# Attention value products: high and low value weights side by side for two query blocks, halves added on VectorE, and an order of its own for the last head pair

## The reference, cut to what matters

```
def one_block(args):
    q_blk, fq_blk, pos_blk = args
    s = jnp.einsum("bqhd,bkhd->bhqk", q_blk, k, preferred_element_type=jnp.float32) * scale
    s = s + fq_blk[..., :, None] - fk_t[:, :, None, :]
    mask = kpos[None, :] <= pos_blk[:, None]
    s = jnp.where(mask, s, -jnp.inf)
    pr = jax.nn.softmax(s, axis=-1)
    return jnp.einsum("bhqk,bkhd->bqhd", pr.astype(v.dtype), v)
```

## Time and profile before

| | us |
|---|---|
| median of 3 runs (2857.04 to 2859.82) | 2859.51 |
| the profiled execution | 2863.89 |
| its span, first to last instruction | 2862.1 |
| attention, first value transposes of pair 0 to those of pair 7 | 584 |
| last pair, from there to the first matmul of the output projection | 77.4 |

### The profile page before, as it was taken

The page is one execution under the profiler, slowest core; times in us unless marked ns, Lnnn a source line. Parts: engine busy times, 40 slices in busy tenths (PEclk is TensorE's granted clock), DMA queues, the critical chain, the costliest instruction groups (busy, mean ns, idle before and its releaser), DMA issues.

```text
span 2862.1 us, 43282 instructions
## 1 busy us (share of the span) xinstructions
PE 2773.8 (97%) x18039; PEld 2699.5 (94%) x18039; DVE 1366.4 (48%) x1841; ACT 835.4 (29%) x1328; POOL 118.4 (4%) x82
## 2 busy tenths in 40 slices
PE   7999999999999999999999999879999999999998
PEld 7999999999999999988888888769999999999998
DVE  7676354244244344455556555554542442442444
ACT  6566221111111122334444444442211111110221
POOL 1000200000000000300000000002000000000000
PEclk9999999999999999999999999889999999999999
DMA  3112111111111111232222233111111111111112
GB/s 133 38 37 90 55 45 44 55 45 38 53 45 42 50 51 38 56 106 83 81 75 70 90 90 97 53 38 46 45 40 51 50 40 54 45 38 53 45 44 78
DMA packets 91341, 166.48 MB, mean 58 GB/s; under 512 B 18066, under 2 KB 55154, under 8 KB 91026
## 3 DMA queue, kind: packets, MB, share of 16 engines
q1 hardware_dynamic: 91154, 163.72, 18.9%
HBM read 141.60 MB, written 13.70 MB: 54 GB/s over the span
## 4 chain that ended last, share of the span: by engine, by line
PE 88%; DVE 4%; issue 4%; ACT 2%; DMA 1%; DVEq 0%; SPq 0%; ACTq 0%
PE psum L339 78%; PE psum L1151 2%; PE psum L1099 2%; PE psum L1123 2%; DVE SB L1551 1%; DMA NF<-nf_scratch 1%; PE psum L1081 1%; DVE PTL L1578 1%; PE psum L1138 1%; ACT PTH L879 0%; DVE X L1634 0%; PE psum L949 0%; ACT L695 0%; ACT SB L863 0%; PE psum L951 0%
## 5 line engine op out<-in xcount | busy, mean ns | idle before, releaser
L339 PE MATMUL psum<-XH,WH 128*128 128x352 f32 x2904 | 642.0, 329 | 1.7 <-issue 1.7
L339 PE MATMUL psum<-XL,WH 128*128 128x352 f32 x2904 | 627.5, 324 | 0.0
L339 PE MATMUL psum<-XH,WL 128*128 128x352 f32 x2904 | 627.1, 323 | 0.0
L321 ACT ACTIVATE WH<-WR 128x1024 fp32r<-128x1024 f32 (+2 forms) x217 | 215.4, 993 | 1037.1 <-PE psum L339 1025.1
L339 PEld LDWEIGHTS psum<-XH,WL 128*128 128x128 f32 x2904 | 498.0, 188 | 1.6
L339 PEld LDWEIGHTS psum<-XL,WH 128*128 128x128 f32 x2904 | 494.0, 188 | 1.6
L339 PEld LDWEIGHTS psum<-XH,WH 128*128 128x128 f32 x2904 | 489.9, 190 | 4.9 <-issue 2.3
L1434 DVE TENSOR_TENSOR X<-psum,X 128x1056 f32<-128x1056 f32 x63 | 79.2, 1258 | 371.1 <-PE psum L339 371.1
L330 DVE TENSOR_TENSOR WL<-WR,WH 128x1024 fp32r<-128x1024 f32 (+2 forms) x217 | 246.1, 1134 | 12.0 <-ACT WH L321 11.6
L339 PE MATMUL psum<-FYH,WH 128*128 128x352 f32 x1134 | 245.3, 324 | 0.0
L339 PE MATMUL psum<-FYH,WL 128*128 128x352 f32 x1134 | 244.4, 323 | 0.0
(11 more groups left out here) (226 smaller groups left out, 3273.9 us busy)
## 6 DMA issues: line engine op xcount, KB each, us to landing
WR<-in_wfi SPq DMA_DIRECT2D x96, 512.0 KB, 3.5
WR<-in_wfo SPq DMA_DIRECT2D x64, 384.0 KB, 3.1
WR<-in_wa SPq DMA_DIRECT2D x24, 512.0 KB, 3.6
WR<-in_wqkv SPq DMA_DIRECT2D x24, 512.0 KB, 4.5
X<-in_xT SPq DMA_DIRECT2D x16, 528.0 KB, 5.0
CC<-in_ck SPq DMA_DIRECT2D x128, 64.0 KB, 1.8
NF<-nf_scratch SPq DMA_DIRECT2D x16, 512.0 KB, 4.8
CC<-in_cv SPq DMA_DIRECT2D x128, 64.0 KB, 1.9
```

The lines of the kernel that those rows point to most:

```text
L321: nc.scalar.activation(WH[:, par, 0:n], WR[:, par, 0:n], ACT.Copy).then_inc(w_hi, 1)
L339: mm = nc.tensor.matmul(psum[0:m, 3 * slot + c, 0:CH], w, x[:, k, c * CH:(c + 1) * CH], start=(k == 0 and part == 0), stop=(k == nk - 1 an ...
```

## The change

Three things change, all in attention.

**Products.** `VV` holds for each key block the four pieces low of head 0, high of head 0, high of head 1, low of head 1, of 64 columns each, so the high and low values of one head lie side by side as 128 columns of weights. `PTH` and `PTL` hold two units side by side. `BLOCKS` is now 7, 6, 1, 0, 5, 4, 3, 2 (sizes 8, 7, 2, 1, 6, 5, 4, 3), so that units 2d + 1 and 2d + 2 are neighbouring query blocks. `product(d)` takes both at once: per key block two matmuls (`PTH`, `PTL`) with 128 columns of weights and 256 of queries, and for the last key block, which only the higher query block has, 128 of queries. The output has 128 rows, high and low halves of the same 64 outputs; its place is one half of the PSUM bank `O_ps`, in turns. ACT copies one 64-row half to `X` (sets `o_half`) and DVE adds the other to it (`add_halves`, sets `o_read`). The product now also includes low by low.

**Places in the order.** There are 8 products in a pair and not 16. `product(d)` stands in PE's step 2d + 4 before `turn(2d + 3)`; it waits for `o_read` up to `add_halves(d - 1)`. On DVE `add_halves(d - 1)` stands in step 2d + 4 behind max(2d + 4). The decode product stands before `turn(1)`. `KSTEPS` is dealt out anew (24 in all again), and the scaling of the k projection moves on DVE from step 13 to step 12.

**The last pair.** Even units are transposed into `T_alt` (the idle first accumulator), odd ones into `T_ps`, so a turn waits for the low part of two units back. On PE `logits(v + 1)` stands ahead of `turn(v - 1)`; on DVE max(v) stands ahead of the scaling of v - 1, and the low part of v - 2 follows. The second head's bias goes to a place of its own, `NF_last`, and is loaded without waiting for max(8).

The diff, cut to its core:

```
-BLOCKS = [7, 0, 6, 1, 5, 2, 4, 3]
+BLOCKS = [7, 6, 1, 0, 5, 4, 3, 2]
-KSTEPS = [2, 1, 2] + [1] * 14 + [3, 2]
+KSTEPS = [2, 1, 1, 1, 2, 1] + [1] * 6 + [2, 1, 1, 1, 1, 2, 2]
+PVS = 1 + NQB
...
+        def t_unit(c, v):
+            return T_alt if c == NHP - 1 and v % 2 == 0 else T_ps
...
+        def o_double(d):
+            return O_ps[:, 2 * P * (d % 2):2 * P * (d % 2 + 1)]
...
# SP
+                if last:
+                    sp.wait_ge(k_out, 16 * NHP)
+                else:
+                    sp.wait_ge(s_read, u0 + 1 + NQB)
+                sp.dma_start((NF_last if last else NF)[:, :], ...)
...
# ACT
+                        if v >= 4 and v % 2 == 0:
+                            act.wait_ge(pv_done, PVS * c + v // 2 + 2 * PVS * t)
+                        nc.scalar.activation(pt_unit(PTH, v - 1), t_blocks(c, v - 1), ACT.Copy)
+                    elif v >= 5 and v % 2:
+                        d = (v - 5) // 2
+                        act.wait_ge(pv_done, PVS * c + d + 2 + 2 * PVS * t)
+                        nc.scalar.activation(out_double(d, hp), o_double(d)[HALF[1 - h], :], ACT.Copy).then_inc(o_half, 1)
...
# PE
+                def product(d):
+                    v = 2 * d + 2
+                    pe.wait_ge(pt_lo, (UNITS - 1) * c + v + 2 * (UNITS - 1) * t)
+                    wait(pe, o_read, NQB * c + d + 2 * NQB * t if c or d else 0)
+                    for kb in range(i + 2):
+                        b = 0 if kb <= i else 1
+                        for y, part in ((PTH, 0), (PTL, 1)):
+                            mm = nc.tensor.matmul(o_double(d)[:, P * b:2 * P], vv, y[:, kb, b:2, :], ...)
...
+                    if v == 2:
+                        decode_product()
+                    elif v >= 4 and v % 2 == 0:
+                        product((v - 4) // 2)
                     if 1 <= v <= UNITS:
                         turn(v - 1)
-                    if v >= 2:
-                        product(v - 2)
...
# DVE
+            def add_halves(c, t, d):
+                dve.wait_ge(o_half, PVS * c + d + 2 + 2 * PVS * t)
+                nc.vector.tensor_tensor(x, o_double(d)[HALF[h], :], x, ALU.add).then_inc(o_read, 1)
...
+                    if v < UNITS:
+                        maximum(v)
+                    if v >= 6 and v % 2 == 0:
+                        add_halves(c, t, (v - 6) // 2)
```

More of the change, by code:

```diff
@@ L850, in pair @@
                     keys_hi(0, 0, 0)
-                for v in range(UNITS + 2):
+                for v in range(UNITS + 3):
                     if v == 2:
@@ L1062, in values @@
                     wait(pe, pt_lo, (UNITS - 1) * (c + 2 * t))
-                    wait(pe, o_read, u0)
                     for kb in range(NQB):
@@ new lines, in decode_product @@
+                def decode_product():
+                    pe.wait_ge(pt_hi, u0 + 1)
+                    pe.wait_ge(vn_rd, c + 1 + 2 * t)
+                    nc.tensor.matmul(O_ps[:, 0:2 * NS], VN[:, :], PTD[0:NS, 4 * NS:6 * NS],
+                                     start=True, stop=False, skip_group_check=True)
+                    for b in range(DB):
+                        pe.wait_ge(cc_ld[b], 32 * (2 * c + 2) + 128 * t)
+                        for g in range(NPG):
+                            cols = slice(2 * NS * g + 2 * DS * b, 2 * NS * g + 2 * DS * (b + 1))
+                            mm = nc.tensor.matmul(O_ps[:, 2 * DS * b:2 * DS * (b + 1)],
+                                                  CC[:, b, PAGE * g:PAGE * (g + 1)], PTD[:, cols],
+                                                  start=False, stop=(b == DB - 1 and g == NPG - 1),
+                                                  skip_group_check=True)
+                    mm.then_inc(pv_done, 1)
@@ L1144, in product @@
+                def product(d):
+                    v = 2 * d + 2
                     h, i = UNIT_OF[v]
                     pe.wait_ge(pt_lo, (UNITS - 1) * c + v + 2 * (UNITS - 1) * t)
-                    pe.wait_ge(o_read, u0 + v)
-                    cols = slice(HD * h, HD * (h + 1))
-                    for kb in range(i + 1):
-                        keys = slice(P * kb, P * (kb + 1))
-                        for x, y, part in ((VH, PTH, 0), (VH, PTL, 1), (VL, PTH, 2)):
-                            mm = nc.tensor.matmul(O_ps[0:HD, 0:P], x[:, kb, cols], y[v % 2][:, keys],
-                                                  start=(kb == 0 and part == 0), stop=(kb == i and part == 2))
@@ new lines, in product @@
+                    mm.then_inc(pv_done, 1)
+                if last:
+                    logits(0)
+                    values()
+                    logits(1)
+                    for v in range(1, UNITS + 2):
+                        if v + 1 < UNITS:
+                            logits(v + 1)
+                        if v == 2:
+                            decode_product()
+                        if v <= UNITS:
+                            turn(v - 1)
+                        if v >= 4 and v % 2 == 0:
+                            product((v - 4) // 2)
+                    return
@@ new lines, in pair, with maximum @@
+                    add_halves(c - 1, t, NQB - 1)
+                def maximum(v):
+                    rows, n = (2 * NS, DK) if v == 0 else (P, P * (UNIT_OF[v][1] + 1))
+                    bias = DM if v == 0 else NF_last if c == NHP - 1 and v > NQB else NF
+                    wait(dve, t_done, u0 + max(v - 1, 0))
+                    if v in (1, 1 + NQB):
+                        dve.wait_ge(nf_ld, 16 * (2 * c + 1 + (v > 1)) + 64 * t)
+                    wait_apart(dve, qk_done, u0 + v + 1, logits_seen)
+                    nc.vector.tensor_tensor_reduce(
+                        SB[0:rows, v % 2, 0:n], S_ps[0:rows, 0:n], bias[0:rows, 0:n],
+                        -SCALE, 3.0e38, ALU.add, ALU.min, nmax[0:rows, v:v + 1]).then_inc(s_read, 1)
@@ new lines, in normalise @@
+                def normalise(v):
+                    rows, n = (2 * NS, DK) if v == 0 else (P, P * (UNIT_OF[v][1] + 1))
+                    dve.wait_ge(e_done, u0 + v + 1)
+                    nc.vector.reciprocal(linv[0:rows, v:v + 1], lsum[0:rows, v:v + 1]).then_inc(rl_done, 1)
+                    dve.wait_ge(rl_done, u0 + v + 1)
+                    nc.vector.tensor_scalar(SB[0:rows, v % 2, 0:n], SB[0:rows, v % 2, 0:n],
+                                            linv[0:rows, v:v + 1], None, ALU.mult).then_inc(p_norm, 1)
```

197 lines of the change are left out of this document (102 added, 95 removed).

## The result

| | median us | span of the profiled execution | mean pair of 0 to 6 | last pair |
|---|---|---|---|---|
| before | 2859.7 | 2862.1 | 83.5 | 77.4 |
| after | 2892.3 (2892.2 to 2894.8, 4 runs) | 2893.0 | 89.0 | 72.0 |

The ratio is 1.0115, with a 95% interval of 1.0099 to 1.0131. The change makes the kernel 32.7 us slower. I had forecast 14.3 us slower: the sign and the range (2850 to 2896) held, the size did not.

A forecast was written before the change was run, and what follows sets the result against it. It took TensorE to bound pairs 0 to 6, with VectorE's chain close behind. Seven pairs at +3.5 us (+24.5) and the last pair's -10.2 make +14.3 on 2859.5: 2874 us, range 2850 to 2896.

The forecast's parts named there:

- The matmuls: TensorE's products in a pair: 8.3 us for 13.0, 4.7 us less work, with 256-column matmuls starting 0.115 apart.
- What bounds the pair: Pairs 0 to 6: TensorE, with VectorE's chain close behind; TensorE's waits in attention about 4 us a pair.
- The serial step: Even steps 10 to 16 run maximum, addition, product, turn, high part, low part serially: +4.8 us a pair.
- The first part and the end of a pair: Stretch from max(3) to max(8) +0.5 us (0 to +1.5); end of a pair, after unit 15's low part, -1.8.
- the forecast's case: Pairs 0 to 6 grow 3.5 us each, +24.5, and the last pair falls 10.2: 2874 us; chance 0.58.
- rival 3: TensorE's longer idle stretches ahead of products bring 1.2 GHz more often: two to three us more a pair, 2892; chance 0.15.
- rival 1: At product(d)'s wait for the addition: the waits are hidden, each pair gains 4.7 us, 2816; chance 0.13.
- rival 2: The waits in a pair are half hidden: it grows by 1.5 us only, 2860, no change; chance 0.11.
- Rival 4: In the products, loading 128 weight columns for each 256 isn't hidden: 4.8 us a pair, 2912; chance 0.03.
- The last pair: The last pair, 77.4 us: -12, -2 and -1 against additions +2.8 and waits +2, sum -10.2 (-5 to -16).
- the own order: In the last pair: maximum ahead of scaling lets exp run under the maximum, -12 us; the NF wait goes, -2.
- The copy at the end: End of the last pair, before the output projection: ACT's weight copy can go while the addition runs, -1 us.

The follow-up runs named there:

- e9: The changed kernel without the addition of the halves, in the last pair too; 2840.9 us, ratio 0.9937.
- e5: The kernel before with the new block order and the last pair's own order, second transpose home and early NF load, old products, no additions; 2837.2 us.
- e1: The changed kernel with half copy and addition of halves one step earlier in pairs 0 to 6, last pair as changed; 2848.4 us.
- e12: The changed kernel with the turn ahead of the product again in pairs 0 to 6, the addition left in place; 2866.7 us.
- e6: The changed kernel with 24, 10, 14 and 18 unread small matmuls in TensorE's waits at products 3 to 6, pairs 0 to 6; 2883.3 us.
- e7: The kernel before, its order and one block a product kept, but with 128-column weights, half copies and additions; 2907.2 us.
- e4: The kernel before with the change's order of query blocks and nothing else; 2851.7 us, ratio 0.9971.
- e15: The kernel of e1 with the turn ahead of the product in pairs 0 to 6; 2850.9 us.
- e14: The kernel of e6 with unread small matmuls in the last pair's waits too; 2877.3 us.

## Why the prediction was right, and where it was wrong

**The matmuls: right in the difference.** The 256-column matmuls start 0.12 apart for my 0.115, and the products take 5.4 us a pair less in e9 than in e5, where I had 4.7. Both sides were priced too low, the new products at 8.3 for 9.6 and the old at 13.0 for 15.0, and the difference forgives it. A part of it is the 16 matmuls with 128 columns of data: I let them start 0.06 apart, though the turns of the earlier trace rows, as wide in weights and data, are 0.11 apart; in the trace of after they start 0.06 and 0.11 apart in turns. The figure of 81 ns from the Trainium skill, "TensorE: Matmul & The Clock Gate", "Back-to-back issue gap", by which the saving would be twice that, is not what these streams do: they run at 0.060 with 64 columns of weights and at 0.112 with 128.

**What bounds the pair: right, from a reading that is not.** "About 4 a pair" for TensorE's waits spreads the last pair's over all eight. Pairs 0 to 6 have 16.3 us of these waits, 2.3 a pair, and the last pair some 17. TensorE thus had less slack to take up a longer step than I wrote.

**The serial step: right as a mechanism, by e1, e9 and e12.** Its price was forecast as 18.0 for the four even steps and 12.3 for the three odd ones. The odd ones are 12.3. The even ones are 19.9, and 18.8 with the clock mended (e6). So the forecast of 30.3 for max(10) to the low part was 1.8 short: 1.0 is the clock of product 6, nearly all in step 16 (5.51 for my 4.2), and 0.8 is spread over the four steps; I take it for the handing on between engines, which I had put at 0.3 for all four.

**The first part and the end of a pair: right.** I had +0.5 and -1.8. The stretches up to max(10) are +0.4 (0.4 + 0.8 - 0.8), the end is -1.6 (12.03 to 10.46). That the first comes out is in part luck: the new order gives 0.7 between max(8) and max(10), which I had at nothing.

**The step that failed** is the pricing of the forecast's case at full clock, with nothing for the clock: I treated it as a rival of its own, at 0.15, instead of as a term of the sum. I had worked out waits of 2 us ahead of products in a kernel whose last pair, with such waits, shows a clock of 0.79, and then priced product 6 at full speed. The measured case is both at once: a pair is +5.5, of it +3.7 by the serial steps (my 3.5) and +1.8 by the clock (rival 3 had 2.5). Seven times 1.8 is 12.6 us, two thirds of the miss of 18.4. That rival 3's total, 2892, is the measured time is luck: its clock term is larger than the measured one, and the last pair's shortfall fills the gap. Rivals 1, 2 and 4 did not happen. Rival 4's doubt was placed at the wrong matmuls: loads of 128 columns are hidden behind 256 columns of data, and not behind 128 (e7).

**The last pair** is -5.4 for my -10.2. By terms: the own order -13.6 (I had -14, which is in part luck: VectorE's waits for exp, 15.7 us in e4, are 0.5 in e5 for my 12 that go, its maxima wait 6.7 us for turns that I had at nothing, and 17.3 us less are at 1.2 GHz), the additions with their waits +5.1 (72.0 to 66.9 in e9; I had +4.8), the new order of blocks -2.9 (I had nothing). The copy at the end gave nothing for my -1; the first matmul of the output projection waits as long as in the earlier trace rows:

```profile
1939.21 0.63 PE L359 MATMUL psum<-YH,WH 128*128 128x352 f32 x1 [4.06 <-DVE YL L1685]
```

The term that was missing is the pairing itself, 66.9 in e9 against 60.9 in e5: +6.0. I had let it go at nothing, since the product "isn't last here". The clock is where most of it lies: e9 and after have 31 us of this pair at 1.2 GHz, e5 15.7. The price of that can be read from kernels whose last pair is the same program. e1 and e15:

```profile
1823.20:1893.20 70.00, 47.12 (x266) 39.07 (x263) 43.45 (x98) 33.81 (x70) 0.00 (x0) 0.83 0.17 49
```

```profile
1820.80:1895.80 75.00, 53.09 (x263) 45.04 (x263) 43.51 (x98) 33.84 (x70) 0.00 (x0) 0.71 0.16 46
```

e12, after and e6 lie between, 70.9, 72.0 and 73.3 us at 0.80, 0.78 and 0.77. e15 has 42.8 us at 1.2 GHz and e1 24.5: 5.1 us for 18.3, 0.28 each. By that, 4.2 of the 6.0 are the clock. This is worked out, not tried, but e14 bears it out: with 18.0 us at 1.2 GHz for 31.2 of after and 34.4 of e6 it got back 3.2 and 4.4, where 0.28 each makes 3.7 and 4.6. By the same price 4.8 of the own order's 13.6 are the clock too. For the rest of the 6.0 the trace of e9 shows the tie that e15 showed: ScalarE's high part waits for the product 18.4 us in 7 times in this pair, and nowhere in e5's. What this costs by itself no run tells.

In before this pair's long wait over the decode product was one of VectorE for a high part, 9.4, and I wrote that it stays. It stays, as a wait of VectorE's maximum for turn(1), which stands behind the decode product now:

```profile
DVE SB L1608 <- PE psum L1149: 12.3, 7, 8.2
```

Over all: 38.6 in seven pairs and -5.4 in the last, and -2.3 in the parts of the program that are alike in both traces, make the 30.9 between the two spans. The wait that "can't be loosened" because of a bank's two halves was not tried, so the Trainium skill's rule in "PSUM — Partial Sum Buffer", "PSUM bank collisions raise a hardware error", has no evidence here either way; e1 shows that one need not loosen it, only have the addition done earlier.

## What to carry to other kernels

A small operation on a shared result belongs in the step in which its engine waits anyway, not in the step in which its consumer starts: eight additions of 0.42 us cost 7.7 us a pair in one place, with what they do to the clock, and 0.7 in the other. Where a chain's sum makes TensorE wait in every step, price the work behind the waits at both levels of its clock, in the forecast itself. And a change of several parts is to be measured by part: here two of the parts gain 22 us together and the third, the one that was to save matmuls, takes 55 back.

## What the runs showed of the hardware that I had not expected

- With float32 operands the width of the weights sets the pace of short matmuls. The rows of e7 show 0.112 us from start to start for 128 columns of weights and 128 of data, where 64 columns of weights and 128 of data have 0.060, and 128 of weights and 256 of data 0.120. The trace of before had it already: the 32 matmuls of the decode product have 128 columns of weights and only 8 of data, and start 0.112 apart. The bf16 matmuls added in e6, 128 columns of weights and of data, start 0.056 apart. The first row is before, the second e6:

```profile
1509.16 3.74 PE L1138 MATMUL psum<-PTD,CC 128*128 128x8 f32 x32
```

```profile
1374.81 1.51 PE L1177 MATMUL psum<-identB 128*128 128x128 bf16 x24
```

  The Trainium skill, "TensorE: Matmul & The Clock Gate", "LDWEIGHTS (loading the stationary operand)", has the load's time in ns as its columns divided by 1.2, 107 for 128 and 53 for 64, whatever the rows. The float32 rows agree; the bf16 row, with a load and a matmul every 56 ns, does not.
- Work nobody reads can make a kernel faster: 66 small matmuls a head pair, 0.056 us apart, took 9 us off the time (2892.3 to 2883.3), with 34 us less at 1.2 GHz in pairs 0 to 6.
- The same 72 us of program took 70.0 to 75.0 us in five kernels that differ only ahead of it, at granted clocks of 0.83 to 0.71. A difference of 2 or 3 us in such a stretch of one profile is not yet one of the program.
- An order of query blocks that puts two large and two small ones side by side, with no other change, gave 8.6 us (0.9971, interval 0.9961 to 0.9980), where I had expected none.
